# Gate and up weights with four neighbouring rows per partition, two ring places filled by one 4 MB transfer

## The reference, cut to what matters

```python
def ec_moe(h, w_router, w_gate, w_up, w_down):
    cap = EC_FACTOR * T // N_EXPERTS                      # 32
    aff = softmax(h @ w_router)
    wts, tok = top_k(aff.T, cap)                          # per expert
    xs = h[tok]                                           # 32 x 1024
    hid = silu(xs @ w_gate[e]) * (xs @ w_up[e])           # 32 x 2048
    y = hid @ w_down[e] * wts                             # 32 x 1024
    return zeros_like(h).at[tok].add(y)
```

## Time and profile before

| what | us |
|---|---|
| median of three runs | 1713.62 |
| lowest, highest run | 1712.37, 1715.26 |
| span of the profiled execution | 1711.1 |
| TensorE matmul busy | 1397.3 (82%) |
| VectorE busy | 536.3 (31%) |
| ScalarE busy | 389.7 (23%) |
| GpSimd busy | 132.3 (8%) |
| hardware DMA queue busy, mean of 16 engines | 76.8% of the span |

### The profile page before, as it was taken

One profiled execution on the slowest core, in us unless ns is written; L12 is line 12 of the kernel. 1 busy time (PEld: TensorE's weight loads), 2 busy tenths in 40 slices (PEclk: granted clock), 3 DMA queues, 4 the chain that ended last, 5 costly groups with the idle time before them and its releaser, 6 DMA issues.

```text
span 1711.1 us, 21197 instructions
## 1 busy us (share of the span) xinstructions
PE 1397.3 (82%) x8724; PEld 855.2 (50%) x8724; DVE 536.3 (31%) x899; ACT 389.7 (23%) x579; POOL 132.3 (8%) x108
## 2 busy tenths in 40 slices
PE   4999997676666667757766766898999999999999
PEld 2986542222122112212221221476899998989997
DVE  2785310000000000000000000058365557835554
ACT  3515200000000000000000000057443346843332
POOL 1430000000000000000000000004500000730000
PEclk8999988877878877787877787899999999999999
DMA  9777599999999999999999999992154544425552
GB/s 376 263 290 301 228 382 426 429 427 429 429 429 429 429 428 429 429 428 428 428 429 428 428 429 429 428 344 99 52 195 179 178 162 149 143 99 197 195 179 93
DMA packets 80325, 542.05 MB, mean 317 GB/s; under 512 B 6312, under 2 KB 9721, under 8 KB 52626
## 3 DMA queue, kind: packets, MB, share of 16 engines
q1 hardware_dynamic: 76912, 535.93, 76.8%
q0 software_dynamic: 1632, 5.03, 1.0%
q10 hardware_dynamic: 1730, 0.36, 0.1%
HBM read 540.22 MB, written 1.08 MB: 316 GB/s over the span
## 4 chain that ended last, share of the span: by engine, by line
PE 47%; DMA 47%; DVE 3%; ACT 1%; issue 1%; POOL 1%; SPq 0%; DVEq 0%; ACTq 0%; POOLq 0%
DMA ring<-in_w_down 22%; DMA ring<-in_w_up 21%; PE bank L1387 10%; PE bank L1389 10%; PE bank L1388 10%; PE bank L1754 4%; PE bank L1773 3%; PE bank L1640 2%; DMA ring<-in_a_w_in 2%; DMA ring<-in_w_mod 1%; DMA ring<-in_w_in 1%; PE bank L1423 1%; PE bank L1621 1%; PE bank L1561 1%; PE bank L1733 1%
## 5 line engine op out<-in xcount | busy, mean ns | idle before, releaser
L1754 PE MATMUL bank<-ring,low 128*32 128x512 f32 x2016 | 314.5, 769 | 152.1 <-DMA ring<-in_w_up 125.7
L1754 PEld LDWEIGHTS bank<-ring,low 128*32 128x32 f32 x2016 | 66.6, 130 | 381.0 <-DMA ring<-in_w_up 192.5
L1773 PE MATMUL bank<-ring,low 128*32 128x512 f32 x976 | 167.7, 822 | 93.7 <-DMA ring<-in_w_down 86.6
L1133 ACT ACTIVATE low<-bank 128x512 f32<-128x512 f32 x16 | 9.6, 597 | 844.8 <-PE bank L1754 844.8
L927 ACT ACTIVATE ring_parts<-ring 128x4096 fp32r<-128x4096 f32 (+3 forms) x46 | 151.9, 3301 | 205.8 <-DMA ring<-in_mlp_w_down 101.0
L2083 DVE TENSOR_TENSOR ring_parts<-ring,ring_parts 128x4096 fp32r<-128x4096 f32 (+2 forms) x35 | 148.5, 4244 | 141.0 <-ACT ring_parts L927 141.0
L1388 PE MATMUL bank<-feat_parts,ring_parts 128*128 128x256 f32 x640 | 181.6, 284 | 0.0
L1389 PE MATMUL bank<-feat_parts,ring_parts 128*128 128x256 f32 x640 | 181.6, 284 | 0.0
L1387 PE MATMUL bank<-feat_parts,ring_parts 128*128 128x256 f32 x608 | 173.4, 285 | 6.8 <-DVE feat_parts L2153 3.7
L2429 DVE TENSOR_TENSOR low<-low,bank 128x512 f32<-128x512 f32 x16 | 11.0, 688 | 462.4 <-PE bank L1754 462.4
L1773 PEld LDWEIGHTS bank<-ring,low 128*32 128x32 f32 x976 | 31.7, 131 | 210.2 <-DMA ring<-in_w_down 135.3
(11 more groups left out here) (407 smaller groups left out, 1979.9 us busy)
## 6 DMA issues: line engine op xcount, KB each, us to landing
ring<-in_w_gate SPq DMA_DIRECT2D x64, 2048.0 KB, 25.7
ring<-in_w_up SPq DMA_DIRECT2D x62, 2048.0 KB, 23.0
ring<-in_w_down SPq DMA_DIRECT2D x61, 2048.0 KB, 26.2
ring<-in_mlp_w_up SPq DMA_DIRECT2D x16, 2048.0 KB, 7.8
ring<-in_mlp_w_down SPq DMA_DIRECT2D x16, 2048.0 KB, 7.9
ring<-in_w_mod SPq DMA_DIRECT2D x11, 2048.0 KB, 15.5
ring<-in_w_in SPq DMA_DIRECT2D x3, 2048.0 KB, 13.3
ring<-in_a_w_in SPq DMA_DIRECT2D x3, 2048.0 KB, 16.1
```

The source lines that it names most:

```text
L1754: last = pe.matmul((GATE if i < 4 else UP)[32 * j:32 * j + 32, :], xsT[:, k, :], held(n, 2)[:, kk, 512 * j:512 * j + 512], start=(k == 0), ...
L1773: last = pe.matmul(TURN[32 * g:32 * g + 32, :], hidT[:, c, 32 * j:32 * j + 32], down_row(n, c, d), start=(j == 0 and c < 2), stop=(j == 3 ...
```

## The change

Gate and up get four neighbouring rows on a partition instead of two (`four_rows`), so that 512 rows are one block of 32 KB per partition. In expert 0 each half of such a block is still a chunk and a transfer of its own: a partition reads 16 KB out of every 32 KB. From expert 1 on `stream_expert` issues one transfer of 4 MB for two chunks (`rides(n)` is true for the second of them, which has no transfer). It waits for the last user of the second place, fills two neighbouring places and counts on the semaphore of the first. Down chunks stay as they were. `RING` becomes (1, 2, 3, 4, 5, 0), with the early places renamed one to one, so that the places of a pair are neighbours. As places are now filled a different number of times per expert, `loads_each(n)` gives TensorE the factor for its waits.

The gather reads `xn` with a stride of four floats. The factors are brought into the new order by 16 products of 32 columns instead of eight of 64, and the five `keep_clock` calls behind them are gone. The two copies into `AB2` keep their size.

```diff
-EARLY = SLOTS - 2
+EARLY = 1
-        RING = (4, 5, 2, 3, 0, 1)
+        RING = (1, 2, 3, 4, 5, 0)
+        PAIRED = 8
+        def rides(n):
+            return FIRST_EXP + PER_EXP <= n < FIRST_SPLIT and (n - FIRST_EXP) % PER_EXP in range(1, PAIRED, 2)
         def loads(n):
+            if rides(n):
+                return loads(n - 1)
...
+        def loads_each(n):
+            at = n - rides(n)
+            return 16 * sum(1 for m in range(PER_EXP) if slot(FIRST_EXP + PER_EXP + m) == slot(at)
+                            and not rides(FIRST_EXP + PER_EXP + m))
...
             def expert_src(e, i):
                 if i < 8:
-                    w = I["w_gate" if i < 4 else "w_up"][0, e, 2 * P * (i % 4):2 * P * (i % 4 + 1), :]
+                    return four_rows(e, i)[:, 2 * (i % 2):2 * (i % 2) + 2, :]
+            def four_rows(e, i):
+                w = I["w_gate" if i < 4 else "w_up"][0, e, 4 * P * (i % 4 // 2):4 * P * (i % 4 // 2 + 1), :]
+                return w.rearrange("(p k) n -> p k n", p=P)
+            def stream_expert(e, first, turn=0):
+                for i in range(PER_EXP):
+                    n = first + i
+                    if i >= PAIRED:
+                        stream(n, expert_src(e, i), turn=turn)
+                    elif i % 2 == 0:
+                        sp.wait_ge(chunk_used, last_user(n + 1, slot(n + 1)) + turn)
+                        sp.dma_start(ring[:, slot(n):slot(n) + 2, :].rearrange("p a (k n) -> p (a k) n", k=2), four_rows(e, i))\
+                            .then_inc(slot_full[slot(n)], 16)
...
-            for v, vec in enumerate((A2, B2)):
-                for kk in range(2):
-                    for half in range(2):
-                        last = pe.matmul(bk("ab2")[64 * half:64 * half + 64, 8 * v + 4 * kk:8 * v + 4 * kk + 4], ident[:, kk::2],
-                                         vec[:, half::2], start=True, stop=True)
+            for r in range(4):
+                for u in range(4):
+                    last = pe.matmul(bk("ab2")[32 * u:32 * u + 32, 4 * r:4 * r + 4].rearrange("p (v k) -> p v k", v=2),
+                                     ident[:, r::4], AB[:, :, u::4], start=True, stop=True)
             end(last, "ab2")
             banks.wait_free(pe, "affT")
-            keep_clock(bk("affT"), 5)
...
-                                         xn[:, t, 2 * P * (k // 2) + k % 2:2 * P * (k // 2 + 1):2],
+                                         xn[:, t, 4 * P * (k // 4) + k % 4:4 * P * (k // 4 + 1):4],
...
-                    need(n, turn)
+                    need(n, turns * loads_each(n))
```

More of the change, by code:

```diff
@@ L213, in two_blocks @@
         A1 = sb("A1", [P, 2, KD])
-        A2 = sb("A2", [P, KD])
-        B2 = sb("B2", [P, KD])
+        AB = sb("AB", [P, 2, KD])
+        A2, B2 = AB[:, 0, :], AB[:, 1, :]
         AB2 = sb("AB2", [P, 2, KD])
@@ L368, in two_blocks @@
         early_split = list(proj.values())
-        early_slots = {proj["a"]: 0, mods[1, 0]: 1, proj["q"]: 2, mods[1, 1]: 3, proj["k"]: 0, mods[1, 2]: 1, mods[1, 3]: 3,
-                       mods[2, 0]: 0, mods[2, 1]: 1, proj["v"]: 2, mods[2, 2]: 5, mods[2, 3]: 3, wo1[0]: 0, wo1[1]: 1}
-        early_slots.update((mods[0, kp], kp) for kp in range(4))
+        early_slots = {proj["a"]: 5, mods[1, 0]: 0, proj["q"]: 3, mods[1, 1]: 4, proj["k"]: 5, mods[1, 2]: 0, mods[1, 3]: 4,
+                       mods[2, 0]: 5, mods[2, 1]: 0, proj["v"]: 3, mods[2, 2]: 2, mods[2, 3]: 4, wo1[0]: 5, wo1[1]: 0}
+        early_slots.update((mods[0, kp], (5, 0, 3, 4)[kp]) for kp in range(4))
         extra = (mid, big[:, 0:SLOT], feat)
@@ L405, in loads @@
                 return slot_full[X_REST], 16 * len(REST)
-            return slot_full[slot(n)], 16 * sum(1 for m in range(n + 1) if slot(m) == slot(n))
+            return slot_full[slot(n)], 16 * sum(1 for m in range(n + 1) if slot(m) == slot(n) and not rides(m))
+        def loads_each(n):
+            at = n - rides(n)
+            return 16 * sum(1 for m in range(PER_EXP) if slot(FIRST_EXP + PER_EXP + m) == slot(at)
+                            and not rides(FIRST_EXP + PER_EXP + m))
         def last_user(n, s):
@@ L685, in expert_src @@
                 if i < 8:
-                    w = I["w_gate" if i < 4 else "w_up"][0, e, 2 * P * (i % 4):2 * P * (i % 4 + 1), :]
-                else:
-                    w = I["w_down"][0, e, 4 * P * (i - 8):4 * P * (i - 7), :]
+                    return four_rows(e, i)[:, 2 * (i % 2):2 * (i % 2) + 2, :]
+                w = I["w_down"][0, e, 4 * P * (i - 8):4 * P * (i - 7), :]
                 return w.rearrange("(p k) n -> p k n", p=P)
+            def four_rows(e, i):
[10 more added lines that the diff above has]
+                            .then_inc(slot_full[slot(n)], 16)
             def rest_piece(i):
@@ L716, in _ @@
                     rest_piece(1)
-            for i in range(PER_EXP):
-                stream(FIRST_EXP + PER_EXP + i, expert_src(1, i))
+            stream_expert(1, FIRST_EXP + PER_EXP)
             with sp.Fori(2, N_EXP) as e:
-                for i in range(PER_EXP):
-                    stream(FIRST_EXP + 2 * PER_EXP + i, expert_src(e, i), turn=(e - 2) * PER_EXP)
+                stream_expert(e, FIRST_EXP + 2 * PER_EXP, (e - 2) * PER_EXP)
             for n in range(FIRST_SPLIT, first_mlp[0]):
@@ L1727, in _, with expert @@
             banks.wait_all_free(pe, "experts", [1])
-            def expert(e, first, turn, last_one=False):
+            def expert(e, first, turns, last_one=False):
                 pe.wait_ge(sem("slots"), e + 1)
@@ L1788, in _ @@
             with pe.Fori(1, N_EXP - 1) as e:
-                expert(e, FIRST_EXP + PER_EXP, (e - 1) * (16 * PER_EXP // SLOTS))
-            expert(N_EXP - 1, FIRST_EXP + PER_EXP, (N_EXP - 2) * (16 * PER_EXP // SLOTS), last_one=True)
+                expert(e, FIRST_EXP + PER_EXP, e - 1)
+            expert(N_EXP - 1, FIRST_EXP + PER_EXP, N_EXP - 2, last_one=True)
             keep_clock(MISC, 5)
@@ L2395, in _ @@
             for v in range(2):
-                dve.tensor_copy(AB2[:, v, :].rearrange("p (i k) -> p k i", k=2),
-                                bk("ab2")[:, 8 * v:8 * v + 8].rearrange("p (k i) -> p k i", k=2))\
+                dve.tensor_copy(AB2[:, v, :].rearrange("p (i r) -> p r i", r=4),
+                                bk("ab2")[:, 0:16].rearrange("p (r v i) -> p r v i", r=4, v=2)[:, :, v, :])\
                     .then_inc(*((sem("ab2"), 1) if v == 0 else (banks.drain_sem("ab2"), 1)))
```

## The result

The changed kernel took 1718.55 us (median of 6 runs, 1716.39 to 1720.90); the kernel before, beside it, 1713.63. The ratio is 1.0029, with a 95% interval of 1.0019 to 1.0040. The prediction was 1710.3 with a range up to 1715.8. It was wrong in its sign and outside its range. (What lies around the span is 1.8 us here, not the 2.5 that were taken; the difference that was forecast doesn't hang on it.)

What follows compares the result with a forecast made beforehand. The prediction took the experts' stage as bound by DMA transfers, bytes over rate. Its terms, -5.0 (G) + 0.5 (B) + 1.2 (T) = -3.3 us, took 1713.62 to 1710.3 us; the 8-in-10 range was 1705.5 to 1715.8.

Steps and rivals of the forecast that it cites:

- G: Gate and up transfers of 15 experts: 32 KB packets, half as many, save per-packet cost; 5.0 us faster.
- (a): Gate and up transfers get no larger packets, so no rate gain; 1715.3 us; chance 0.13.
- (c): Gate and up transfers: higher cost per packet, so the gain is 9.1 us; 1706.2 us; chance 0.14.
- (d): Partitions read at a distance of 32 KB, gate and up rate falls, 13 us more; 1728.6 us; chance 0.06.
- The queue in steady state: DMA queue during the experts: pairs issued later still leave some 9.9 us of margin, so no cost.
- (e): DMA queue runs dry once per expert; at 1 us each 1725 us; chance 0.05.
- B: Hand-over from expert 0 to expert 1: a hole in the queue, 0 to 1.5 us, taken as 0.5 us slower.
- The router: TensorE's chain ahead of the experts: the gather's stride of four costs 0 to 0.3 us, taken as 0.
- (f): The gather's loads double, a gather of 7.7 us delaying the start by 3.85; 1714.2 us; chance 0.04.
- The five calls: Router: removing five `keep_clock` calls, with products added, changes nothing, since TensorE waits for `aff` either way.
- T: End of the last expert: first down chunk 2.7 us late, less about 1.5 us of slack; 1.2 us slower.
- (b): Last expert's up chunks meet the slow clock, so the end costs 2.9 us; 1712.0 us; chance 0.13.

Runs made afterwards that it cites:

- e4: The changed kernel with the gather at a stride of two floats and the five `keep_clock` calls back: 1710.33 us.
- e5: The changed kernel with the gather at stride two, the `keep_clock` calls back and each half block its own 2 MB transfer, no pairs: 1712.61 us.
- e1: The kernel before with only the gather's stride changed, from two floats to four: 1719.12 us.
- e3: The changed kernel with the five `keep_clock` calls put back ahead of the wait for `aff`: 1718.12 us.
- e7: The changed kernel with the calls back, VectorE writing the normed input in the weights' order, and expert 1 in single transfers: 1710.96 us.
- e9: The changed kernel with the calls back, VectorE writing the normed input in the weights' order, and expert 15 in single transfers: 1709.92 us.
- e11: As e9 (expert 15 in single transfers), but ScalarE forms the second half of the turned input: 1708.60 us.

## Why the prediction was wrong, point by point

**The rate (G = 5.0).** Right in mechanism and size: 32 KB packets, and 4.1 us in the changed kernel, 4.9 in e4, by bytes moved in the middle. e5 shows that it is the pairs and not the order in memory, and the packet times show 12.5 ns saved where I had 11.8. Rivals (a), (c) and (d) fall.

**The queue in steady state.** Right: up pairs land 20.6 us after their issue, 9.8 of them their own two steps, which leaves 10.8 us of margin where I had 9.9, and from 300 to 1080 us no stretch of 60 us lies under 429 GB/s. Rival (e) falls.

**The holes at the hand-over (B = 0.5).** About right when TensorE isn't late: e4 moved 385 GB/s from 260 to 265 us where e5 moved 419, which is 0.4 us; but from 255 to 275 us both moved the same (428 and 427 GB/s), so B lies between 0 and 0.4. In the changed kernel the hole was 2.6 us, because expert 1 began 5.6 us late and its first chunks ran at the lower clock. I had tied B to the time at which TensorE reaches expert 1 but had not asked what a slow gather does to it.

**The router: the step that failed.** I wrote that the stride of four costs "0 to 0.3 us; I take 0", since the transposes' loads, which have a stride of four, took 212 ns against 196 for the gather's with two. These are different instructions. The transposes without a stride, in the view by line of the kernel before (203 to 228 us), say what 212 has to be held against:

```profile
L1358 PEld LDWEIGHTS bank<-con,x x16: 138/141/143, 204.0 to 206.3; 128*128 128x128 f32 x16
```

141 to 212 is half as much again, in a group of four where nothing waits for it. Like against like, the trace bore the rule out; I gave it 0.04. The Trainium skill (Advanced Engine Details and Errata, section Memory Cachelines) asks for two hits on a line of 16 bytes; here strides of one, two and four floats took 192, 196 and 329 ns, and the measurement agrees. Rival (f) named this mechanism and priced it at 3.9 us, once. It comes twice: the gather of expert 0 holds back the first free place, and the gather of expert 1 the fourth pair. e1 measures 6.1 us for both, and 7.8 with pairs (e3 against e4).

Neither I nor rival (f) saw that the slow gather also brings the lower clock. In e1, whose only edit is the stride, the granted clock averaged 0.67 to 0.81 in all sixteen gathers; in the kernel before it was 0.88 to 1.00 in fifteen and 0.50 in one. Behind the gather of expert 1 it stood at 0.50 in e1, e3 and the changed kernel alike from 265 to 270 us, and the first two chunks took 2.0 us longer in the changed kernel. The lower clock comes there without the stride too, but less: in e4 it averaged 0.73 from 260 to 265 us.

**The five calls.** I set their removal at nothing since TensorE waits for `aff` anyway. The time was covered, the clock was not: in that wait the calls were what kept TensorE busy. This is the second, smaller error, 1.0 us by the trace and from nothing to 0.7 in the medians.

**The end (T = 1.2).** The mechanism is there: the first down chunk starts 7.5 us after the start of the last pair (1103.89 to 1111.39), 7.7 predicted, and VectorE's first half result begins 0.04 us ahead of ScalarE's start on `a_w_in` instead of 1.15. But the second half ended 2.93 us behind that start, as before (2.91): the delay just fitted in the slack. I had carried 2.7 us through to the sums. 2.5 were there at the first down chunk, and 1.1 at the half result, for that chunk took 1.92 us where it had taken 3.31: the lower clock had passed. Only e3 and e7 show a cost in their traces (3.95 and 4.90 us), and in both the first chunk of the last up pair ran at the lower clock (3.49 and 3.64 us instead of 1.92). That is rival (b), with 1.0 and 2.0 us where it had 2.9. So T was mis-sized, 0 in most traces, and the medians of e9 to e11 leave it between 0.1 and 0.7 us.

**The sum.** With the stride and the calls undone the kernel takes 1710.33 us, 2.7 under the kernel before beside it. The agreement with the 1710.3 and the -3.3 of the sum is partly luck. The terms as the traces show them give -4.9 + 0.4 + 0 = -4.5; e4's profiled execution took 1709.17 us, 3.8 under the median of the kernel before; e4's own median lies 1.2 us higher, and the cause of that stays open. The interval of e4's median is 1.5 us to either side.

## What to carry to other kernels

A layout that gives the DMA larger pieces moves the stride somewhere else; price every reader of the turned operand by rows of the same instruction at the new stride, and put the turning on an engine that has time. In a kernel bound by transfers, look at the few places where the queue is empty: in this kernel each us of a compute chain was paid there in full, and with larger transfers, which are issued later, it is paid again at the next hand-over. Products that nobody reads need not be free to remove because the engine waits at that point; ask what clock the work behind the wait gets. The same question goes for an operation that becomes slower: here the strided gather took the chunks behind it to the lower clock.

## What the runs showed of the hardware

A load of 128 columns from a stride of four floats goes at a pace that TensorE's clock doesn't set. In the changed kernel the gather took 7.67 or 7.68 us in every expert but the first (7.57), with the granted clock at 0.50 throughout (at 781 us) or at a mean of 0.66 (at 257 us). With a stride of two it took 3.96 us at 1.00 (at 256 us) and 7.03 at 0.50 (in the last expert of the kernel before). So the strided load costs 0.6 us more where the clock is low, and nearly doubles the time where it is high. First the changed kernel, then the kernel before:

```profile
781.01:788.68 7.67, 7.67 (x35) 7.67 (x34) 0.00 (x0) 0.00 (x0) 0.00 (x0) 0.50 1.03 444
257.44:265.12 7.68, 7.68 (x35) 7.68 (x34) 0.00 (x0) 0.00 (x0) 0.00 (x0) 0.66 0.97 402
```

```profile
1069.17:1076.20 7.03, 7.03 (x35) 7.03 (x34) 0.00 (x0) 0.00 (x0) 0.00 (x0) 0.50 0.99 420
255.61:259.57 3.96, 3.96 (x36) 3.96 (x34) 0.00 (x0) 0.00 (x0) 0.00 (x0) 1.00 1.03 420
```

Reading a stride of four floats and writing contiguously, 128 x 1024 floats took VectorE 1.15 us against 0.75 without the stride. On ScalarE the strided copy took 2.12 us, and the nearest operation without a stride, a square of the same size, 1.05.
